# One fused two-block kernel: a split first product, a new order of products in the second block's mixers, split last products

## The reference

```python
p = u @ w_in[l]
p_pool, p_bval, p_bgate, p_cgate, p_cx = jnp.split(p, splits, axis=-1)   # 256, 256, 256, 512, 512 columns
y_a = _pool_mixer(p_pool, pool_w[l], pool_scale[l])
y_b = _conformer_conv(p_bval, p_bgate, ...)      # value * sigmoid(gate), 31 taps in time, layernorm, silu, 256x256
y_c = _rglru_branch(p_cgate, p_cx, ...)          # 4 taps in time, two gates (sigmoid), a linear scan, times gelu(cgate)
y = jnp.concatenate([y_a, y_b, y_c], axis=-1)
h = h + y @ w_out[l]
u = _rmsnorm(h, mlp_norm_g[l])
h = h + jnp.square(jax.nn.relu(u @ w_up[l])) @ w_down[l]
return _rmsnorm(h, final_norm_g)[:, N_META:]
```

## Time and profile before

| | us |
|---|---|
| median of 3 runs | 1062.16 |
| lowest, highest | 1058.67, 1063.05 |
| the profiled execution | 1063.24 |
| its span, first to last instruction | 1061.5 |

### The profile page before, as it was taken

The page is one execution under the profiler, slowest core; times in us unless marked ns, Lnnn a source line. Parts: engine busy times, 40 slices in busy tenths (PEclk is TensorE's granted clock), DMA queues, the critical chain, the costliest instruction groups (busy, mean ns, idle before and its releaser), DMA issues.

```text
span 1061.5 us, 12504 instructions
## 1 busy us (share of the span) xinstructions
PE 1028.4 (97%) x4959; PEld 861.5 (81%) x4959; DVE 508.7 (48%) x828; ACT 421.6 (40%) x657; POOL 573.6 (54%) x712
## 2 busy tenths in 40 slices
PE   6999999999999999999999878999999999999996
PEld 5888888888888888888899767888788888888884
DVE  2782356665356633545676797457113213212332
ACT  5353345555624424433336653353212212212231
POOL 3555546556556754565644885364555554555540
PEclk9999999999999999999999988899999999999998
DMA  6223222122442215332312202322323232322312
GB/s 221 85 81 118 80 80 81 41 79 80 121 157 80 80 48 186 107 120 80 102 59 79 80 26 74 100 80 80 119 80 119 80 119 80 113 86 80 119 40 80
DMA packets 91403, 98.61 MB, mean 93 GB/s; under 512 B 3234, under 2 KB 86720, under 8 KB 91344
## 3 DMA queue, kind: packets, MB, share of 16 engines
q1 hardware_dynamic: 91344, 97.81, 28.4%
HBM read 95.71 MB, written 2.10 MB: 92 GB/s over the span
## 4 chain that ended last, share of the span: by engine, by line
PE 86%; DVE 9%; ACT 4%; DMA 0%; issue 0%; SPq 0%; DVEq 0%; ACTq 0%
PE ps L321 77%; PE ps L663 1%; DVE ps L1112 1%; PE ps L644 1%; PE ps L788 1%; DVE Hl L428 1%; PE ps L601 1%; PE ps L603 1%; DVE tmp L1528 1%; DVE Fm L1076 1%; PE ps L1037 1%; DVE Fm L1026 1%; DVE tmp L406 1%; PE ps L395 1%; DVE Al L1470 1%; PE ps L366 1%
## 5 line engine op out<-in xcount | busy, mean ns | idle before, releaser
L245 POOL TENSOR_TENSOR wlo<-raw,whi 128x256 fp32r<-128x256 f32 x672 | 512.3, 794 | 404.6 <-ACT whi L240 404.6
L321 PE MATMUL ps<-Hh,whi 128*128 128x512 f32 x848 | 338.4, 399 | 8.2 <-DVE Hl L1191 3.3
L321 PE MATMUL ps<-Hl,whi 128*128 128x512 f32 x848 | 334.4, 394 | 0.0
L240 ACT ACTIVATE whi<-raw 128x1024 fp32r<-128x1024 f32 x168 | 177.0, 1054 | 163.4 <-PE ps L321 157.9
L321 PE MATMUL ps<-Hh,wlo 128*128 128x512 f32 x848 | 214.4, 392 | 0.8 <-POOL wlo L245 0.8
L321 PE MATMUL ps<-Ah,whi 128*128 128x512 f32 (+1 forms) x576 | 197.8, 366 | 0.5 <-DVE Fm L406 0.3
L321 PEld LDWEIGHTS ps<-Hh,whi 128*128 128x128 f32 x848 | 161.6, 191 | 43.6 <-DVE Hl L1191 3.8
L321 PE MATMUL ps<-Al,whi 128*128 128x512 f32 (+1 forms) x576 | 195.1, 361 | 0.0
L321 PEld LDWEIGHTS ps<-Hh,wlo 128*128 128x128 f32 x848 | 160.8, 190 | 35.1 <-POOL wlo L245 1.2
L321 PEld LDWEIGHTS ps<-Hl,whi 128*128 128x128 f32 x848 | 161.7, 191 | 33.3 <-issue 0.5
L321 PE MATMUL ps<-Ah,wlo 128*128 128x512 f32 (+1 forms) x576 | 124.1, 360 | 0.0
(11 more groups left out here) (269 smaller groups left out, 907.8 us busy)
## 6 DMA issues: line engine op xcount, KB each, us to landing
raw<-in_w_in SPq DMA_DIRECT2D x36, 1024.0 KB, 5.3
raw<-in_w_up SPq DMA_DIRECT2D x16, 1024.0 KB, 5.3
raw<-in_w_down SPq DMA_DIRECT2D x16, 1024.0 KB, 5.0
raw<-in_w_att_out SPq DMA_DIRECT2D x4, 1024.0 KB, 5.0
raw<-in_w_sg_out SPq DMA_DIRECT2D x4, 1024.0 KB, 4.9
raw<-in_w_o SPq DMA_DIRECT2D x4, 1024.0 KB, 5.0
Fm<-in_x SPq DMA_DIRECT2D x2, 1024.0 KB, 6.3
Fm<-in_x SPq DMA_DIRECT2D x1, 2048.0 KB, 8.5
```

Of the source, the lines that this page charges most:

```text
L240: eh = A(lambda e, s=s, src=src, kk=kk: e.activation(wtile(whi, s, kk), src, ACT.Copy), raw_ev[b], used)
L245: el = G(lambda e, s=s, src=src, kk=kk, cut=cut: e.tensor_tensor(wtile(wlo, s, kk)[:, *cut], src[:, *cut], f(wtile(whi, s, kk))[:, *cut], ...
L321: return e.matmul(ps[:, bk, 0:c1 - c0], wt, x[:, k, c0:c1], start=st, stop=sp)
```

## The change

It has three parts.

1. **Start.** The first weight block (1 MB) is loaded as two halves by rows (k-slices 0 to 3 and 4 to 7), each behind a half of x. Sixteen matmuls of ones, whose result nobody reads, run on PE first. The first product begins when k-slices 0 to 3 of x and weights are ready; in its middle stand the transposes and splits of k-slices 4 to 7, the conversion of the second half, and the squares for the norm. The second weight block waits for x.
2. **Mixers.** The products come as gate 0, value 0, cx 0, cx 1, gate 1, value 1, cx 2, cx 3. Two of the gate and two of the value tiles are loaded as blocks of one tile (512 KB, rows of 512 bytes). The pieces of `mixers` are dealt anew: the 31-tap list of the first channel half opens behind the second product instead of the fifth, `rg_conv` and the high part (`rg_high`) are apart, the gates of the recurrence come one piece earlier behind cx 3, and the scaling of the first pool product (`pool_in`) stands ahead of two of the four low parts.
3. **End.** The last two down products are computed in two halves of 256 tokens each, in the order (6, first), (7, first), (6, second), (7, second), with half-width adds, squares, sums, factors and stores, so that the first half's two output tiles are scaled and stored under the second half's product.

```diff
-        cols("w_in_2", 0, 1280, 1)
-        cols("w_in_2", 0, 512, 1)
-        cols("w_in_2", 0, 256, 1)
-        cols("w_in_2", 0, 1536, 1)
+        for i in range(2):
+            cols("w_in_2", 0, 512 + 128 * i, 1, per=1)
+            cols("w_in_2", 0, 256 + 128 * i, 1, per=1)
+            cols("w_in_2", 0, 1280 + 256 * i, 1)
...
+        def load_first(h):
+            nm, r0, c0, kk, per = blocks[0]
+            src = t[nm][0][r0 + 512 * h:r0 + 512 * h + 512, c0:c0 + 256].rearrange("(k p) n -> p k n", p=128)
+            first_raw.append(q.dma("sp", raw_block(0)[:, 4 * h:4 * h + 4], src, d_first[h], *e_x[:h]))
...
+        def first_tile(h):
+            ks = slice(4 * h, 4 * h + 4)
+            src = raw_block(0)[:, ks, 0:128]
+            eh = A(lambda e: e.activation(whi[:, 0, ks], src, ACT.Copy), first_raw[h])
+            for part in range(2):
+                cut = slice(4 * h + 2 * part, 4 * h + 2 * part + 2)
+                el = G(lambda e, cut=cut: e.tensor_tensor(wlo[:, 0, cut], raw_block(0)[:, cut, 0:128],
+                                                          f(whi[:, 0, cut]), ALU.subtract), eh, signal=(part == 1))
+            first_hi.append(eh)
+            first_lo.append(el)
+            if h == 1:
+                hi_ev.append(None)
+                lo_ev.append(None)
+                fed[1] = 1
...
+            if i == 0:
+                load_first(0)
+        load_first(1)
+        raw_ev.append(first_raw[1])
+        fed[0] = 1
+        q.wait("sp", e_x[1])
+        load_block()
...
+        for i in range(16):
+            T(lambda e: e.matmul(ps[:, 2, 0:128], ones[:], ones[:], start=True, stop=True), e_ones, signal=False)
...
+        for k in range(4):
+            x_split(k, x_turn(k))
+            if k == 0:
+                first_tile(0)
...
+        def second_half():
+            nonlocal e_r
+            for k in range(4, 8):
+                x_split(k, x_turn(k))
+                if k == 4:
+                    first_tile(1)
+            feed(2)
...
-        b1, m1 = h_product(3)
+        b1 = one_bank(3)
+        m1 = product([[(b1, 0, 512)]], Hh, Hl, hev, mid=second_half, tail=4)[0]
...
-            cx(0, *made[0])
+            s0 = sgt_scaled(0, *made[0])
...
+            sgt_times(0, s0)
+            rescale(0, 3)
+            yield
+            conv_input(0, *made[1])
+            rescale(3, 5)
+            taps(2, (0,))
+            yield
+            taps(4, (0,))
+            yield
+            cx(0, *made[2])
+            taps(1, (0,))
             rg_conv(0)
-            yield
-            got["R1"] = ended(sp1)
-            rescale(0, 2)
+            rg_high(0)
...
+            conv_input(1, *made[5])
             rg_root(0)
             yield
+            side_taps()
             taps(2, (0,))
             rg_scan(0)
             table(ACT.Sigmoid)
             yield
-            conv_input(1, *made[5])
+            cx(2, *made[6])
             rg_scan(1)
+            rg_conv(2)
+            rg_high(2)
+            rg_low(2)
             yield
             side_taps()
-            taps(2, (1,))
-            yield
-            cx(2, *made[6])
-            taps(1)
-            rg_conv(2)
-            rg_low(2)
-            yield
-            side_taps()
+            taps(1, (1,))
             yield
             cx(3, *made[7])
             taps(1)
+            yield
+            rg_gate(2, 0)
             rg_conv(3)
+            rg_high(3)
             rg_low(3)
-            yield
             side_taps()
             yield
-            rg_gate(2, 0)
+            rg_gate(2, 1)
             scale_cg(0)
             taps(1)
             yield
-            rg_gate(2, 1)
+            rg_gate(3, 0)
+            rg_input(2)
             side_taps()
             taps(1)
             yield
-            rg_gate(3, 0)
+            rg_gate(3, 1)
             scale_cg(1)
-            rg_input(2)
-            taps(1)
-            yield
-            rg_gate(3, 1)
             rg_exps(2)
             taps(1)
...
+            cg_lo((0, 1))
+            yield
+            pool_in(0, *made[8])
+            cg_lo((2, 3))
+            ea = pool_mix(0)
+            yield
...
-            for n in range(8):
+            for n in range(8 if part < 3 else 6):
...
+            order = [(k, whi, x) for k in range(8) for x in (Hh, Hl)] + [(k, wlo, Hh) for k in range(8)]
+            for i, (k, w, x) in enumerate(order):
+                q.wait("pe", *acts[k], lo_ev[j] if w is wlo else None)
+                ev = T(lambda e, i=i, k=k, w=w, x=x: e.matmul(
+                    ps[:, bk, 0:256], wtile(w, s, 8)[:, k], x[:, k, 256 * h:256 * h + 256], start=(i == 0),
+                    stop=(i == 23)), signal=(i == 23))
+            return bk, ev
...
+        run_half(6, 0)
         while bgs:
             finish(bgs[0])
-        R4 = sm[:, 180:184]
-        e_R4 = factors(R4)
-        d_out = dsem("d_out")
-        for i in range(4):
-            if i == 3:
-                ev = A(lambda e: e.activation(OT[:, 3, :], OT[:, 3, :], ACT.Copy, scale=R4[:, 3:4]), e_R4, *ot_ev)
-            else:
-                ev = V(lambda e, i=i: e.tensor_scalar(OT[:, i, :], OT[:, i, :], R4[:, i:i + 1], None, ALU.mult), e_R4,
-                       *ot_ev)
-            e_out = q.dma("sp", out_v[:, i, :], OT[:, i, :], d_out, ev)
+        row_ot = [list(ot_ev), list(ot_ev)]
+        run_half(7, 0)
+        next(turns[6, 0], None)
+        run_half(6, 1)
+        er = half_factors(0, half_sums(0))
+        next(turns[7, 0], None)
+        b7 = half_product(7, 1)
+        next(turns[6, 1], None)
+        half_out(0, er)
+        turns[7, 1] = half_turn(7, 1, *b7)
+        next(turns[7, 1])
+        em = half_sums(1)
+        next(turns[7, 1], None)
+        e_out = half_out(1, half_factors(1, em))
```

162 lines of the change are left out of this document (115 added, 47 removed).

## The result

| | us |
|---|---|
| changed kernel, median of 9 runs (lowest, highest) | 1056.53 (1052.97, 1058.55) |
| kernel before beside it, median of 9 runs | 1060.91 (1058.67, 1066.70) |
| ratio, 95% interval | 0.9948 (0.9927 to 0.9968) |
| profiled execution of the changed kernel, its span | 1053.21, 1051.4 |

The change is worth 0.5%, 5.5 us (3.4 to 7.7 by the interval), and not the 13.6 that was forecast; the median lies just above the upper end of the range, 1056.5. The two profiled executions are 10.1 us apart in span, since the one after lies near the lowest of its nine and the one before 2.3 above its own median.

The account below looks back on a forecast made before the run. PE, 86% of the chain that ended last, was taken as the bound, with time to win at the start, in the mixers and after the last product. 2.4 + 7.6 + 3.6 = 13.6 us off 1062.16 gave 1048.5, range 1040 to 1056.5.

Parts of the forecast that it names:

- Start, 2.4 forecast: At the start: the second product begins at 19.9 instead of 22.28, 2.4 us earlier; bounds 3.2 earlier, or nothing.
- The matmuls of ones cost nothing: At the start: they take some 3.1 us, while PE has nothing else until x lands at 6.8.
- Mixers, 7.6 forecast: In the mixers: PE goes on with the output products 7.6 us earlier; bounds 15.3 at best, 2 us more at worst.
- The last sigmoid 8.2 earlier, 2 allowed for new waits, 6.2.: Mixers' gates: 3.5 us wait, 1.8 slow clock and 2.9 from earlier gates go; less 2, the pool scaling moves 6.2.
- no wait for a sigmoid over 1.5 us: Sign in the profile that the forecast is right: PE waits for no sigmoid longer than 1.5 us.
- This chain keeps its length.: Mixers: from the last gate's sigmoid through scan, gelu product and low parts to the first pool scaling, length unchanged.
- 1.4 us less to the second pool low part.: Mixers, from the first pool scaling: DVE has six taps instead of ten, two low parts more: 2.7 - 1.2 = 1.4 us.
- End, 3.6 forecast: After the last product: 5.0 us less, part paid back by PE, 3.1 to 3.6 shorter; bounds 5 shorter or 1 longer.
- The sign of two stores landed before the last matmul: Sign at the end: 7 to 8 us after the last matmul, with two stores landed before it.
- The mixers' waits only move: Rival, mixers: DVE's work is the same and still ends the pool chain; only start and end gain, 6.0: 1056.2; chance 0.15.
- the slower case: Rival, early gates: taps ahead in DVE's queue make gates wait, 5.3 us per gate; five give 1077.4; chance 0.05.
- the second rival: At the start: the first product is not brought forward, the second x half gates as before, nothing gained: 1050.9; chance 0.07.

## Why the prediction was wrong, point by point

**What bounds the kernel.** Right: PE waits at the same three stages, and nothing changed between them (from the convolution's mix to the sixth add of the last MLP part it takes 358.8 to 359.4 us in every trace).

**Start, 2.4 forecast.** The place was right (19.9 forecast; 19.08 to 20.07 found, and its sum for the full clock, 19.1, is what the early ones show), the base was not. 22.28 belongs to executions in which the clock had fallen behind PE's wait for the weights; others reach 19.9 to 20.2 without any change. So the term is a gain of 2 to 3 us in a part of the executions, and 1.4 us with an interval that holds zero when timed; and in the traces it is the matmuls of ones that bring it, not the split (19.07 without it; the split without them was not run). "The matmuls of ones cost nothing" failed too: sixteen take 5.5 to 6.6 us and not 3.1, and in four of six executions with sixteen of them x was turned at 7.4 to 7.9, not at 6.7 to 6.9.

**Mixers, 7.6 forecast: the step that failed.** Of the 8 us that are missing, 6 are here. By its own working:
- *The last sigmoid 8.2 earlier, 2 allowed for new waits, 6.2.* It is 1.7. The 3.5 us wait did not go, it was dealt out again: 2.2 + 0.8 + 0.5 = 3.5 in front of the three gates. The four gates share two banks, and I had followed the one sigmoid that the order moves ahead of the high part; the next one still stands behind it, and the high part behind three taps that took 4.61 us. The slow clock did not go with it: in those traces it falls once ahead of the last gate in either order. The prediction's own sign, no wait for a sigmoid over 1.5 us, failed with the 2.2. What is left is 1.7 of the 2.9 us that half a product less was to give. This is the largest part of the loss, 4.5 us, and little of it is GpSimd's: without the additions the sigmoid moves 2.1. That the wait held it is seen where the side taps are kept off DVE's chain: there the three taps take 3.49 us and no side taps stand ahead of that second sigmoid, the wait is 0.45 us, and the stretch to the last gate 71.94, 1.8 less at an equal clock.
- *"This chain keeps its length."* It grew by 1.85, though it now holds two low parts less (1.2 us). Some 2.1 us of it are GpSimd's additions (4.3 in the new order, 2.2 in the old), beside which DVE's instructions with both operands in SBUF were longer. The other 0.95 is ACT's: DVE's product ahead of the first scan began 8.91 us behind the last gate's sigmoid and begins 9.86 behind it now (607.61 - 597.75), with and without the additions, since ACT now converts a weight tile (L263, 603.35) ahead of the root that this product needs. Before, the tile stood behind it:

```profile
611.26 0.72 DVE L1075 TENSOR_TENSOR Fm<-Fm 128x528 f32<-128x528 f32 x1 [0.93 <-ACT Fm L1071]
...
611.67 1.05 ACT L240 ACTIVATE whi<-raw 128x1024 fp32r<-128x1024 f32 x1
```

That is read from the traces; no run moved the tile alone. The stretch by GpSimd was to be seen before: the same three taps stood at 2.37 and 3.68 us on DVE's timeline, the gelu products at a mean of 1.37 beside low parts at 0.68, and a mean over them was taken for a property of the instruction. The Trainium skill, "SBUF — State Buffer", "Who interferes with whom", states that a DVE instruction with two SBUF inputs contends with a GpSimd instruction that reads SBUF, and that one with at most one SBUF input, outside the 2-port perf modes, does not contend. The trace agrees (1.093 and 0.814 us for the low parts, 0.696 both times for the scaling from PSUM).
- *1.4 us less to the second pool low part.* It is 1.4, in each of three traces, but in part by luck: the two low parts that move in take 1.8 and not 1.2, two of the four taps that go only leave DVE waiting 0.7 us for ACT, and other instructions of the stretch were held up less. Without the additions the two orders differ there by 0.06.
- *The slow clock behind the pool waits stays.* It stays, but differs by 3 us from execution to execution.

**End, 3.6 forecast ("3.1 to 3.6").** Right: 3.1 (0.7 to 5.4) timed, 3.0 to 3.3 by the traces. The tail behind the last product is 7.5 us, 4.9 less than before, and 1.8 is given back ahead of it, as the sum had it (5.0, and at most 1.9). The sign of two stores landed before the last matmul failed: they were issued before it. The halves run at 0.12 us a matmul:

```profile
1030.87 0.28 PE L1623 MATMUL ps<-Hl,whi 128*128 128x256 f32 x1
1030.99 0.28 PE L1623 MATMUL ps<-Hh,whi 128*128 128x256 f32 x1
```

The rule on weight loads of the Trainium skill, "TensorE: Matmul & The Clock Gate", Part 3, with the time of a load that stands in its Part 2, would have made the halves an estimated 5.1 us longer; the rows show no such time.

**The rivals.** "The mixers' waits only move" gave 1056.2 for the reason that held: 12.3 us of waits became 11.9. That its number is met so closely is partly luck, for the start gave less than its 2.4 and the mixers more than nothing. It had 0.15, because 10 idle us of DVE ahead of the gates were counted as room, and what the chain behind them takes was left as it had been. The early gates wait once, 0.5 us (the 0.8 is chunk 2's), far from the slower case; the first product did start early, at 8.95; the halves' loads are hidden.

**The size of the noise.** The sum was made against one execution, and its lost clock (1.8 in the mixers, some 2.3 at the start) was booked as gain, though the runs shown ahead of the change already spread by 4.4 us. The arithmetic holds but for last digits: 1062.16 - 13.6 is 1048.6, and the second rival comes to 1051.0.

## What to carry to other kernels

Before an instruction's duration is put into a sum, look at its spread over the trace: where the same form takes 0.7 and 1.3 us, ask which engine runs beside it in the long case, and whether the change moves it there. A wait is gone only when every instruction that frees its buffer has been followed, not just the one that the order moves. Time that the clock gave in one execution is no term of a sum: take the stages from several. A stretch that waits for DVE alone repeats within 0.1 us here; one that runs at PE's pace, even in part, moves with each fall of the clock and is compared only with one that has as many.

## What the runs showed of the hardware that was not expected

- DVE's instructions with two SBUF operands (128 by 512 or 528, float32) went from 0.68 to 0.70 us up to 1.2 to 1.8 beside GpSimd's additions, and to 1.2 beside its weight parts; a scan went from 1.26 to 2.24. Those with one operand in PSUM stayed at 0.70 to 0.75. The profile shows this as busy time of DVE and not as a wait.
- Removing sixteen additions of GpSimd (26.3 us of its time) gave 10.6 us of the whole by medians of different hours, though GpSimd is busy for little more than half of the span.
- The granted clock falls at different places in different executions of the same program, and not only behind a wait (0.93 from 526 to 550 us, with PE busy for 23.92 of 24): the nine runs of the changed kernel lie between 1052.97 at a mean of 0.995 and 1058.55 at 0.989, and its two traces have the same waits. With 35 matmuls of ones in front of four waits it stayed at 1.00 there in the one execution profiled, and the median was about 3 us lower.
